# Two of three merge branches computed inside the sample attention, a quarter unit per chunk, on one Trainium2 core

## What is computed

```python
ya = fox_attention(q, k, v, ...) * silu(ga)       # (tokens, 512)
yb = rms_norm(gla(...), g_gla) * silu(gb)         # (tokens, 512)
yc = bc * short_conv(cc * xc) * silu(gc)          # (tokens, 512)
gates = sigmoid(mg).reshape(..., 3, D_MODEL)
merged = (gates[:, :, 0] * (ya @ w_branch_a)      # each 512 x 1024
          + gates[:, :, 1] * (yb @ w_branch_b)
          + gates[:, :, 2] * (yc @ w_branch_c))
out = x + merged @ w_out                          # 1024 x 1024, then rms_norm
```

## Time and profile before

| | us |
|---|---|
| median of 3 runs | 3411.84 (3409.48 to 3414.87) |
| the profiled execution | 3416.05 |
| its span, first to last instruction | 3414.3 |
| mean granted clock of PE | 0.983 |

### The profile page before, as it was taken

The page is one execution under the profiler, slowest core; times in us unless marked ns, Lnnn a source line. Parts: engine busy times, 40 slices in busy tenths (PEclk is TensorE's granted clock), DMA queues, the critical chain, the costliest instruction groups (busy, mean ns, idle before and its releaser), DMA issues. The chain is left out here.

```text
span 3414.3 us, 58799 instructions
## 1 busy us (share of the span) xinstructions
PE 3175.8 (93%) x20175; PEld 2455.5 (72%) x20175; DVE 1775.6 (52%) x3118; ACT 1414.2 (41%) x2928; POOL 1044.3 (31%) x991
## 2 busy tenths in 40 slices
PE   7899999999999999999799999888888887999998
PEld 6678887787788778888577777555555555778787
DVE  4425556787756565555566666244444444444432
ACT  4412223454622474654577777422332333211222
POOL 2511313244354535140378788300000000222100
PEclk9999999999999999999799999999999999999999
DMA  7878788788879787878412222699999999554322
GB/s 270 306 229 270 237 253 263 243 317 277 291 249 322 237 292 243 278 239 230 121 38 63 66 66 90 235 386 386 382 388 383 386 385 333 192 167 166 130 88 83
DMA packets 430462, 817.78 MB, mean 240 GB/s; under 512 B 98605, under 2 KB 120021, under 8 KB 430186
## 3 DMA queue, kind: packets, MB, share of 16 engines
q1 hardware_dynamic: 418130, 807.02, 70.1%
q10 hardware_dynamic: 11488, 5.11, 0.6%
q0 software_dynamic: 576, 2.10, 0.2%
HBM read 674.11 MB, written 132.67 MB: 236 GB/s over the span
## 5 line engine op out<-in xcount | busy, mean ns | idle before, releaser
L1495 PE MATMUL prj_z_ps<-prj_w_hi,prj_h_ring 128*128 128x512 f32 x1792 | 724.2, 404 | 12.4 <-DMA prj_h_ring<-hops_scratch 7.3
L1497 PE MATMUL prj_z_ps<-prj_w_hi,prj_h_ring 128*128 128x512 f32 x1792 | 703.6, 393 | 0.0
L1496 PE MATMUL prj_z_ps<-prj_w_lo,prj_h_ring 128*128 128x512 f32 x1792 | 701.7, 392 | 0.0
L1964 POOL TENSOR_TENSOR pa_p_lo<-pa_probs,pa_p_hi 128x512 fp32r<-128x512 f32 (+1 forms) x320 | 368.2, 1170 | 108.0 <-ACT pa_p_hi L1976 104.7
L1495 PEld LDWEIGHTS prj_z_ps<-prj_w_hi,prj_h_ring 128*128 128x128 f32 x1792 | 339.1, 189 | 82.7 <-issue 8.2
L1497 PEld LDWEIGHTS prj_z_ps<-prj_w_hi,prj_h_ring 128*128 128x128 f32 x1792 | 338.2, 189 | 74.9
L1496 PEld LDWEIGHTS prj_z_ps<-prj_w_lo,prj_h_ring 128*128 128x128 f32 x1792 | 339.2, 189 | 66.5
L2645 PE MATMUL sa_t_ps<-arena_ident,arena_k_raw 128*128 128x128 f32 x2048 | 278.7, 279 | 114.9 <-DMA arena_k_raw<-in_cache_k_dram 104.3
L2525 DVE COPY sa_kT<-sa_t_ps 128x512 f32<-128x512 f32 x256 | 177.1, 692 | 355.6 <-PE sa_t_ps L2645 348.0
L2645 PEld LDWEIGHTS sa_t_ps<-arena_ident,arena_k_raw 128*128 128x128 f32 x2048 | 223.5, 141 | 167.2 <-DMA arena_k_raw<-in_cache_k_dram 136.3
L2469 ACT COPY sa_kT<-sa_t_ps 128x512 f32<-128x512 f32 x256 | 150.1, 586 | 444.2 <-PE sa_t_ps L2645 421.2
(11 more groups left out here) (414 smaller groups left out, 6209.0 us busy)
## 6 DMA issues: line engine op xcount, KB each, us to landing
prj_h_ring<-hops_scratch SPq DMA_DIRECT2D x448, 512.0 KB, 4.5
arena_k_raw<-in_cache_k_dram SPq DMA_DIRECT2D x512, 256.0 KB, 5.7
shared_v_early<-in_cache_v_dram SPq DMA_DIRECT2D x260, 256.0 KB, 5.9
sa_v_late<-in_cache_v_dram SPq DMA_DIRECT2D x252, 256.0 KB, 6.0
z_scratch<-prj_z_sb SPq DMA_DIRECT2D x224, 256.0 KB, 5.6
prj_raw<-in_w_main_dram SPq DMA_DIRECT2D x104, 256.0 KB, 5.9
arena_mg<-z_scratch SPq DMA_DIRECT2D x48, 512.0 KB, 4.8
hops_scratch<-prj_h_ring SPq DMA_DIRECT2D x32, 512.0 KB, 5.8
```

Of the source, the lines that this page charges most:

```text
L1495: pe.matmul(out, h[:, 0, k], hi, start=(k == 0), stop=False)
L1496: pe.matmul(out, h[:, 0, k], lo, start=False, stop=False)
L1497: mm = pe.matmul(out, h[:, 1, k], hi, start=False, stop=(k == HK - 1))
L1964: pool.tensor_tensor(p_lo[:, s % P_RING, 0:w], probs[:, s % P_RING, 0:w], p_hi[:, s % P_RING, 0:w].bitcast(F32), ALU.subtract).then_inc(pl ...
```

## The change

`attend_sample` now also computes branches two and three for all 17 tiles, as 34 units of the same 24 products. Each unit is cut into four parts of six products, or three parts of eight (the second unit of every second tile), and one part stands in each of the steps 4 to 131 (`PART_AT`), between `turn(g, 3)` and `weigh(g - 4)`. The units of a tile are gated by DVE, added by POOL (`join`), and ACT stores the sum to a scratch tensor `m_part` and issues all the loads that the units need: the two weights (split in the first four steps), o_gla and its gate, y_c and the two merge gates. To make room in the banks and buffers, the weighted output has one bank, shared with the new tokens' scores, the probabilities have one buffer, and the turned y shares the bank of the turned probabilities. The merge keeps the first branch: 17 units, each gate's result added by POOL onto the loaded sum, and splits four of the slices of w_out between its units (`EARLY`).

The diff, cut to its core:

```diff
--- before.py
+++ after.py
@@ attend_sample
+    UNITS = [(t, i) for t in range(TILES) for i in range(2)]
+    PRODUCTS = [(h, k, a, b) for h in range(NH) for k in range(CH) for a, b in ((0, 0), (0, 1), (1, 0))]
+    PARTS = [3 if i == 1 and t % 2 == 1 else 4 for t, i in UNITS]
+    FIRST_UNIT = 4
+    PART_AT = dict(enumerate(((u, p) for u, n in enumerate(PARTS) for p in range(n)), FIRST_UNIT))
-        probs = m.sb("probs", [P, 2, CK])
+        probs = m.sb("probs", [P, CK])
-        o_ps = m.ps("o_ps", [P, 2, BLK])
+        o_ps = m.ps("o_ps", [P, BLK])
...
+            def join(t, placed):
+                pool.wait_ge(gated, 4 * (t + 1))
+                pool.wait_ge(q_placed, 4 * placed)
+                pool.tensor_tensor(mg[:, 0], mg[:, 0], mg[:, 1], ALU.add).then_inc(joined, 1)
...
+            def branch(g):                                   # ACT
+                if g < FIRST_UNIT:
+                    for x in range(SPLITS * g, SPLITS * (g + 1)):
+                        split(x)
...
+                    if p == 0:
+                        (load_b, load_c)[i](t + 1)
+                    if p == 1 and i == 0 and t > 0:
+                        store_m(t - 1)
+                        load_mg(t, 1)
+                    if p == 2 and i == 0 and t > 0:
+                        load_mg(t, 0)
...
             for g in range(4):
                 load_d(g)
+            load_b(0)
+            for x in range(2 * CH):
+                i, k = divmod(x, CH)
+                act.dma_start(w_raw[:, i, k, 1], branches[i + 1][0, k * P:(k + 1) * P, :]).then_inc(w_loaded[x], 16)
+            load_c(0)
+            load_mg(0, 0)
+            load_mg(0, 1)
             act.wait_ge(pre_turned, 1)
...
+                elif g in PART_AT and PART_AT[g][1] == 0 and PART_AT[g][0] > 0:    # DVE, ahead of reduce(s)
+                    gate(PART_AT[g][0] - 1)
...
                     if x == 0:
-                        wait_from(pe, kept, s - 1)
+                        wait_from(pe, kept, s)
...
+            def turn_y(u, g):
+                t, i = UNITS[u]
+                wait_from(pe, p_ready, min((g - 1) // 2, SEGS))
...
                     turn(g, 2)
                     turn(g, 3)
+                if g in PART_AT:
+                    unit(*PART_AT[g])
+                if last_part(g) and g < max(PART_AT):
+                    turn_y(PART_AT[g][0] + 1 if g in PART_AT else 0, g)
                 if is_chunk(g - 4):
@@ merge_and_project
-    UNITS = [(t, i) for t in range(TILES) for i in range(NB)]
+    ORDER = [*range(CH, KC), *range(CH)]
+    EARLY = {2: 0, 5: 1, 8: 2, 11: 3}
...
+            for t in range(TILES):                           # POOL
+                pool.wait_ge(gated, t + 1)
+                pool.wait_ge(m_loaded[t], 16)
+                pool.tensor_tensor(merged[:, t], merged[:, t], mg[:, t % 2], ALU.add).then_inc(added, 1)
...
+            def load_mg(t):                                  # SP
+                wait_from(sp, added, t - 1)
...
             for t in range(TILES):
                 if t + 2 < TILES:
                     load_a(t + 2)
-                    load_b(t + 2)
+                    load_m(t + 2)
+                    load_mg(t + 2)
+                if t + 1 in EARLY:
+                    load_raw(EARLY[t + 1])
...
+            for u in range(TILES):                           # DVE
+                if u < LAST:
                     low(u + 1)
-                if u + 2 <= LAST_U and u >= 0:
-                    make_y(*UNITS[u + 2])
+                if u + 2 <= LAST:
+                    make_y(u + 2)
+                if u in EARLY:
+                    split_out(EARLY[u])
...
                 gate(u)
```

More of the change, by code:

```diff
@@ L2347, in dims, with out_of, rows_of, tokens @@
             return slice(c * PAIR_D, (c + 1) * PAIR_D)
+        def out_of(s):
+            return o_ps[:, 0:PAIR_D]
+        def rows_of(t):
+            return P if t < PROMPT_TILES else SAMPLE
+        def tokens(t, n=P):
+            return slice(t * P, t * P + n)
+        def last_part(g):
+            u, p = PART_AT.get(g, (-1, 0))
+            return g == FIRST_UNIT - 1 or u >= 0 and p == PARTS[u] - 1
+        x_new, x_turned = o_ps[:, P:P + SAMPLE], o_ps[0:SAMPLE, 2 * P:3 * P]
         def new_rows(n, h):
@@ L2399, in _ @@
             sp.dma_start(arena.in_a[:, 0, 1], z[Z_GA, 0:P, :]).then_inc(arena.a_loaded, 16)
[L2400 to L2403, removed]
+            for k in range(CH):
+                sp.dma_start(arena.branch_a[:, k], branches[0][0, k * P:(k + 1) * P, :]).then_inc(arena.w_loaded[k], 16)
             sp.wait_ge(o_ready, DEC_BATCH)
@@ L2453, in _ @@
             pool.tensor_copy(lift_r[:], lift[:]).then_inc(made, 1)
-            for n in range(1, DEC_BATCH):
-                place(n)
+            place(1)
+            for g in range(G + 4):
+                n, c = divmod(g, CHUNKS)
+                if c == 2 and 1 <= n < DEC_BATCH - 1:
+                    wait_from(pool, joined, sum(1 for x in range(g) if joins_at(x)))
+                    place(n + 1)
+                if joins_at(g):
+                    join(PART_AT[g][0] // 2 - 1, min(DEC_BATCH, 2 + (g - 2) // CHUNKS))
+            join(TILES - 1, DEC_BATCH)
         @block.scalar
@@ L2634, in _ @@
                     divide(n - 1)
+                branch(g)
             dve.wait_ge(arena.a_loaded, 32)
@@ L3168, in project @@
                             mm = pe.matmul(acc[:, t % 2, h], x[:, a, k], wo[:, k, b, h * BLK:(h + 1) * BLK],
-                                           start=(k == 0 and a == 0 and b == 0), stop=(k == KC - 1 and a == 1))
+                                           start=(begin and a == 0 and b == 0), stop=(end and a == 1))
                 mm.then_inc(out_done, 1)
             turn(0)
-            for u in range(len(UNITS)):
+            for u in range(TILES):
                 unit(u)
```

498 lines of the change are left out of this document (282 added, 216 removed).

## The result

The changed kernel takes 3439.63 us (median of 5 runs, 3433.47 to 3445.80), the kernel before 3412.45 beside it (5 runs, 3409.48 to 3419.56): a ratio of 1.0078, 95% interval 1.006 to 1.0096. It is slower by 0.8%, where 3406, some 6 us faster, was forecast. The profiled execution spans 3437.9 us against 3414.3, so 23.6 us are to be found.

The account below looks back on a forecast made before the run. Sample attention was taken as bound by transfers, the merge by PE; 118 + 10 + 10 - 144 - 2 = -8 us, with small adjustments, gave 3406 us. Its own range was 3398 to 3418, the overall range 3380 to 3450.

Parts of the forecast that it names:

- What bounds the kernel: Whole kernel before the change: sample attention bound by transfers at 382 to 388 GB/s, merge and output projection by PE.
- the merge: Branch units: -144 us (-139 to -150); a chain from addition to addition sets 9.75 us a tile, where PE needs 6.03.
- the first addition: Merge: the first addition was to be done 15.5 us after the block's start.
- The end: Sample attention, from the last turned key to the next block: +10 us (+8 to +14), 24.5 us against 14.9.
- the projection: Output projection: -2 us, as four slices of w_out are split before it begins.
- The steady part: Sample attention from chunk 4's first turn to the last turned key: +118 us (+111 to +164), 6.43 us a chunk.
- PE with its waits: Steady sample attention: PE's own 6.21 us a chunk plus 0.11 for two new waits, pacing at 6.32.
- Rival 1: Sample attention: ACT's bulk loads delay keys, PE never makes it up; 6.8 us a chunk, +46, 3452 us; chance 0.28.
- The start: Sample attention's start: +10 us (+6 to +16); 6.0 for 13 issues ahead of q's scaling, 4 for splitting weights.
- Rival 2: Merge: PE falls to 1.2 GHz, 10.8 us a unit, +17, 3423 us; half a unit so stays hidden; chance 0.08.
- the sum of -8: Whole kernel: 118 + 10 + 10 - 144 - 2 = -8 us, a profiled span of 3406 against 3414.3.
- signs of being wrong: Chunks over 6.6 us, merge additions 6 us apart, or over 20 us lost at the sample attention's start.

Follow-up runs that it names:

- experiment 1: Changed kernel, with SP asking in the merge for the operands of tile t+3 before it waits for the addition of tile t: 3388.24 us, ratio 0.9923.
- experiment 11: Changed kernel with two of 24 matmuls in each sample-attention unit and keys asked for ahead of values (branch sums incomplete): 3400.66 us, ratio 0.9958.
- experiment 4: Changed kernel with loads of y_c, branch b's gate and merge gates cut to one row for all tiles but the first: 3410.75 us, ratio 0.9995.
- Experiment 5: Changed kernel with the keys of chunk g+1 asked for ahead of the values of chunk g in the sample attention: 3413.27 us, ratio 0.9992.
- experiment 10: Kernel before the change, with the keys of chunk g+1 asked for ahead of the values of chunk g: 3411.27 us, ratio 0.9996.
- experiment 3: Changed kernel with two of the 24 matmuls in each sample-attention unit, old order of loads (branch sums incomplete): 3430.56 us, ratio 1.0047.
- experiment 2: Changed kernel with q scaled on ACT before the 13 loads are issued, at the sample attention's start: 3429.84 us, ratio 1.0046.
- experiment 9: Changed kernel, six edits: merge operands and w_out slices asked for earlier, q scaled first, first y earlier, keys ahead of values, stores spread: 3327.16 us, ratio 0.9762.

## Why the prediction was wrong

**What bounds the kernel, and the merge: right.** The chain of gate load, operands, y, gate and addition was found in the trace of before and measured within 0.3 us a link; experiment 1 shows that it is the cause. That part missed by 4 us, 2.6 of them in the first addition. The end missed by 1, the projection by 0.5. PE's own 6.22 us a chunk were as worked out.

**The steady part: one term mis-sized.** The step that failed is "I take 6.43: the larger plus 0.06 for the bursts of a tile (1.5 MB of its 2.36 come in two chunks) that the buffers don't take up". The transfers were sized rightly (6.37; 6.39 in experiment 11), PE with its waits a little short (6.32; 6.41 in experiment 4, its own work 6.2 as forecast). What couples them was taken at 0.06 us and measured 6.61 - 6.39 = 0.22, over 124 chunks 20 us more than was allowed for. The step shows as only 16 us in the table because of a second error: 125 chunks were counted where there are 124, which put one chunk, 6.4 us, too much into the forecast. With the right count the sum would have been -14, and the steady part would have missed by 23. The transfers' 385 GB/s had been read in a stretch where SP never stood long at a wait. Experiment 5 gives the cause: a key load stood in SP's order behind the wait for a weighed value, and these waits had grown from 40 to 105 us in 500.

Why they had grown is read from where the value products stand in PE's program. The changed kernel, a unit's part and the value products behind it:

```profile
2864.52 1.64 PE L2926 MATMUL sa_acc<-sa_w,sa_h_parts 128*128 128x512 f32 x6
2867.08 1.08 PE L2895 MATMUL sa_o_ps<-shared_v_early,sa_pT 128*32 128x128 f32 x32 [0.92 <-DVE sa_o_acc L2712]
```

In the kernel before they follow the last turned key of a step at once. Now they start 1.8 us behind it on average and up to 3.5 (over the 500 us from 2400), since the unit's part and the wait for the one output bank stand between, while the next keys' own buffer is free from that turn on. With two matmuls of 24 it is still 1.3 and up to 3.9: PE then waits 32.7 us in 500 for the bank, not 6.1. This fits all six runs: no delay and no cost of the order in the kernel before (against experiment 10), the delay and the cost with PE busy 93% (the changed kernel against 5) and with PE busy 78% (3 against 11). That the delay comes from this place in the program was not tried by itself, for instance with the unit's part behind the value products.

**Rival 1 was half right.** It has the sign, the place (late keys that PE never makes up) and a pace beyond its 6.5. Its mechanism, ACT's bursts ahead of the keys, is not needed for the loss: in experiment 5 the bursts are all there, keys land 2 us later than in the changed kernel, and the pace is 6.43. And in the dip shown the transfers are partly idle, where a burst would fill them. Experiment 4 alone would not have told: with short loads the pace is 6.41 too, with SP still waiting 90.9 us. The spare time of 1.6 us that the rival worked out is of the size of the 1.8 by which the value products now come late; that the one used up the other is a reading, not a measurement.

**The start: mis-sized, beyond its bounds.** 22.8 us against 10 (at most 16). The 13 issues took 2173.81 - 2164.82 = 9.0 us, not 6.0: four of them took 3.15, where 1.85 was read in a stretch with an empty queue. POOL's selects took 1.9 more on top, for which the forecast had nothing. The weights' casts, subtractions and the first y were taken at 4 us; the mark is 11.8 later still than the mask product. PE waited 3.06 and 4.98 for them in sequence, and worked at the lower clock after each. The order of the issues is shown by experiment 2 (13 us); the second part is read from the trace, and only its last 2.3 us were tried (experiment 9).

**Rival 2** came true without its price. PE did fall to 1.2 GHz in the merge, a granted clock of 0.85 from 3060 to 3240. Behind a wait of 4.42 us matmuls stood 0.43 us apart:

```profile
3148.33 0.63 PE L3267 MATMUL mo_acc<-mo_w,arena_h_hi 128*64 128x512 f32 x1
...
3148.76 0.60 PE L3266 MATMUL mo_acc<-mo_w,arena_h_hi 128*128 128x512 f32 x1
3149.18 0.41 PE L3267 MATMUL mo_acc<-mo_w,arena_h_hi 128*64 128x512 f32 x1
```

That lasted 2.3 us in this tile, and in others up to 4.3, less than the half unit (12 x 0.425 = 5.1 us) that the rival let pass. The chain, not PE, set the end. The Trainium skill, "TensorE: Matmul & The Clock Gate", section "HAM oscillation", describes such falls in kernels that wait between bursts; this trace agrees.

Right sign or not, the sum of -8 stood on parts of +138 and -146. Errors of 13 and 16 us in two of five parts, both to the same side, turned it over. Two of its own signs of being wrong came true: a chunk over 6.6 us, and over 20 us lost at the start.

## What to carry to other kernels

When work is moved under a stage that transfers bound, don't add a small allowance for the coupling: look at what the new work stands in front of, which buffers come free later by it, and which loads stand in the issuing engine's order behind the wait for such a buffer without needing it. Put these first (here 22 to 29 us). Work taken out of a stage leaves a chain of handshakes that was hidden; find the load queued behind a wait that it does not need (here 51 us, and 15 more for the next one). An issue is not a constant: take its cost from a stretch in which as much was asked for just before.

## What the runs showed that was not expected

- The rate fell to 144 GB/s in a window of 2 us, where most windows show 382 to 408, after SP had stood at a wait for 5 us.
- Inside the sample attention PE came back from a wait of 1.96 us at half its clock (0.50 from 2552 to 2554), and six matmuls took 1.3 us more. This happened after two of the eight waits of 1.5 us and more in the 500 us; after the other six, of up to 1.92, the granted clock stayed at 1.00.
- Issues on ACT took 0.46 us each into an idle queue, 0.79 each with some 2.6 MB asked for just ahead of them (3.15 for four; 2.0 to 3.3 over the runs), and 0.93 for each of the two gates (0.5 to 1.2).
- Eight selects on POOL took 4.62 us in every profile with q scaled behind the 13 loads, and 2.77 in every other.
- Taking 75 of 466 us of PE's work away moved nothing (experiment 3), while reordering eight issues a chunk did: a busy share of 93% did not say which engine to relieve.
